# PEER experts: the gate pieces and early Gelu rows of pairs 2 and up requested from ScalarE's queue, value and up tiles alone on SyncE's

## The reference, cut to what matters

```python
    def one_block(args):
        xb, ib, gb = args
        u = expert_u[ib]
        a = jax.nn.gelu(jnp.einsum('thkd,td->thk', u, xb).astype(jnp.float32), approximate=False)
        w = (gb * a).astype(expert_v.dtype)
        return jnp.einsum('thk,thkd->td', w, expert_v[ib])
```

## Time and profile before

| | us |
|---|---|
| median of 3 runs | 2859.49 |
| lowest and highest | 2853.49, 2860.74 |
| the profiled execution's own time | 2859.18 |
| its span, first to last instruction | 2857.5 |
| TensorE busy | 2618.8 (92%) |
| VectorE busy | 2137.3 (75%) |
| ScalarE busy | 1347.5 (47%) |
| GpSimd busy | 887.8 (31%) |
| mean granted TensorE clock | 0.960 |
| stage `experts` in the span | about 748 to 1642 |

### The profile page before, as it was taken

How to read it: one execution, slowest core, us unless ns; L and a number is a source line. 1 busy time by engine, 2 the same in 40 slices (tenths; PEclk the granted TensorE clock), 3 DMA queues, 4 the chain that set the end, 5 groups by cost and what they waited for, 6 DMA issues and landing times. The chain is left out here.

```text
span 2857.5 us, 37085 instructions
## 1 busy us (share of the span) xinstructions
PE 2618.8 (92%) x12984; PEld 2188.0 (77%) x12984; DVE 2137.3 (75%) x3830; ACT 1347.5 (47%) x2125; POOL 887.8 (31%) x732
## 2 busy tenths in 40 slices
PE   4899989999999999999999969988898799999993
PEld 3656768888877999999988848857677688888883
DVE  4657658989677988888888866366434799999994
ACT  3224543547533333333333344343342688888882
POOL 2300024765433666554555510001000311122210
PEclk8999999999999999999999979999998899999997
DMA  7730011546899999999999922223222999999993
GB/s 238 263 119 1 30 61 60 181 142 240 317 314 323 356 368 368 372 349 352 349 350 353 329 70 89 89 89 107 89 69 74 295 399 381 370 373 371 366 357 117
DMA packets 278982, 681.49 MB, mean 238 GB/s; under 512 B 57892, under 2 KB 111908, under 8 KB 275752
## 3 DMA queue, kind: packets, MB, share of 16 engines
q1 hardware_dynamic: 219704, 480.26, 47.2%
q0 software_dynamic: 55664, 176.23, 17.3%
q10 hardware_dynamic: 3456, 23.07, 2.0%
HBM read 648.75 MB, written 55.84 MB: 247 GB/s over the span
## 5 line engine op out<-in xcount | busy, mean ns | idle before, releaser
L3381 ACT ACTIVATE ex_w_hi<-expert_raw 128x1024 fp32r<-128x1024 f32 x384 | 376.1, 1072 | 46.7 <-DMA expert_raw<-in_w 24.8
L2100 PE MATMUL bank<-v_hi,peer_w_hi 128*128 128x512 f32 x768 | 302.2, 394 | 12.5 <-DVE peer_w_lo L2203 12.4
L2075 POOL DMA_INDIRECT got_rows<-in_u_rows,diff x160 | 240.2, 1501 | 229.3 <-DVE got_rows L2169 192.0
L3427 DVE TENSOR_TENSOR ex_w_lo<-expert_raw,ex_w_hi 128x1024 fp32r<-128x1024 f32 x256 | 296.5, 1217 | 7.8 <-ACT ex_w_hi L3381 6.2
L2100 PE MATMUL bank<-v_lo,peer_w_hi 128*128 128x512 f32 x768 | 301.0, 392 | 0.0
L2100 PE MATMUL bank<-v_hi,peer_w_lo 128*128 128x512 f32 x768 | 300.6, 391 | 0.0
L2075 POOL DMA_INDIRECT got_rows<-in_expert_v,diff x160 | 218.2, 1364 | 201.5 <-DVE peer_acc L2174 154.4
L2088 PE MATMUL bank<-h_hi,u_hi 128*128 128x352 f32 x736 | 239.8, 326 | 8.4 <-PEq L94 4.9
L2088 PE MATMUL bank<-h_hi,u_lo 128*128 128x352 f32 x736 | 238.5, 324 | 0.0
L2088 PE MATMUL bank<-h_lo,u_hi 128*128 128x352 f32 x736 | 237.7, 323 | 0.0
L2141 ACT ACTIVATE v_hi<-v_in 128x1024 fp32r<-128x1024 f32 x128 | 133.0, 1058 | 211.5 <-PE bank L2100 117.4
(11 more groups left out here) (548 smaller groups left out, 6597.1 us busy)
## 6 DMA issues: line engine op xcount, KB each, us to landing
expert_raw<-in_w SPq DMA_DIRECT2D x384, 512.0 KB, 8.2
v_in<-in_expert_v SPq DMA_DIRECT2D x128, 512.0 KB
u_in<-in_u_tiles SPq DMA_DIRECT2D x118, 512.0 KB
ada_in<-in_w_ada SPq DMA_DIRECT2D x48, 512.0 KB, 4.9
ring<-in_w_in SPq DMA_DIRECT2D x11, 2048.0 KB, 8.6
gates_by_key<-spread ACTq DMA_DIRECT2D x20, 1024.0 KB, 8.3
gate_in<-gates_by_key SPq DMA_DIRECT2D x320, 64.0 KB
ring<-in_w_out SPq DMA_DIRECT2D x4, 2048.0 KB, 8.4
```

Of the source, the lines that this page charges most:

```text
L2075: pool.indirect_dma_start(out=got[:, n % RINGS, :], out_offset=None, in_=table, in_offset=bass.IndirectOffsetOnAxis(ap=rows_at[:, n % ROWS ...
L2100: last = pe.matmul(g.bank[2 + o][:, :], x[:, par, e, i * P:(i + 1) * P], v[par][:, e, c], start=(first and n == 0), stop=(final and i < FU ...
L3381: act.activation(hi[kind][:, c, :], raw_piece(raw, u * PIECES + c), ACT.Copy).then_inc(s["r_hi"], 1)
L3427: dve.tensor_tensor(lo[which][:, c, :], raw_piece(raw, u * PIECES + c), hi[which][:, c, :].bitcast(F32), ALU.subtract).then_inc(s["r_lo"], 1)
```

## The change

`gates_in` and `gel_ready` move out of the SyncE block and take the engine as an argument. SyncE still requests them for pairs 0 and 1. For pair `q + 2` they are requested by ScalarE at the end of its turn `q`, behind both `peer_w_hi` of pair `q`. The wait for `j_w` is gone, because ScalarE has at that point already waited for the same count.

```diff
+            def gates_in(eng, q):
+                for b in range(NB - 1):
+                    eng.dma_start(gate_in[:, q % 2, b], gates[b, :, q * GT:(q + 1) * GT, :]).then_inc(s[f"j_g{q % 2}"], 16)
+                eng.dma_start(gate_last[:, q % 2], last_gate[:, q * GT:(q + 1) * GT, :]).then_inc(s[f"j_g{q % 2}"], 16)
+
+            def gel_ready(eng, q):
+                eng.dma_start(gel_in[:, q % 2], early_gel[q * GT:(q + 1) * GT].rearrange("e p t -> p e t")).then_inc(s[f"j_e{q % 2}"], 16)
+
             @block.sync
...
-                def gates_in(q):
-                    if q >= 2:
-                        sp.wait_ge(s["j_w"], (q - 1) * GT)
...
                 early.saved(sp, EARLY)
-                gel_ready(0)
+                gel_ready(sp, 0)
                 last_gates(sp)
-                gates_in(0)
+                gates_in(sp, 0)
                 for q in range(1, Q):
                     down_in(q)
-                    gates_in(q)
-                    if q < EQ:
-                        gel_ready(q)
+                    if q == 1:
+                        gates_in(sp, q)
+                        gel_ready(sp, q)
                     if EQ <= q < Q - AHEAD:
                         up_in(q + AHEAD)
...
                         if EQ <= q < Q - AHEAD:
                             act_u(act, q + AHEAD, e)
+                    if q + 2 < Q:
+                        gates_in(act, q + 2)
+                    if q + 2 < EQ:
+                        gel_ready(act, q + 2)
                     if q == HALFWAY - 1:
```

## The result

The changed kernel takes 2873.37 us (median of 5 runs, 2870.11 to 2877.24), the kernel before 2858.57 in the same comparison (2853.49 to 2860.74). The ratio is 1.006 with an interval of 1.0043 to 1.0077: **slower by 0.6%**, some 15 us. The forecast was 2869, range 2855 to 2883. One execution of a later variant, behind_tiles, took 5328 us instead of some 2869 and is left out of its ratio.

A forecast was written before the change was run, and what follows sets the result against it. Early pairs were taken as bound by a loop through ScalarE, VectorE and value tiles, late pairs by full TensorE and VectorE. 2859.18 + 9.7 us of early ScalarE issuing, all else zero, gave 2869 us, range 2855 to 2883.

The forecast's parts named there:

- Case A: Early pairs: ScalarE's issuing closes the loop, 9.5 us a pair against 8.91, +9.7 us in all; chance 0.60.
- The block: Early pairs: seven requests on ScalarE between second `peer_w_hi` and first `v_hi`, taken as 3.7 us.
- The second part: Early pairs: from first `v_hi` to the next pair's second `peer_w_hi`, 5.7 us.
- The upper end of the block: Early pairs: the seven requests take 5 us if pieces cost 0.7 us, as when the queue is full.
- The loop before: Early pairs before the change: loop through ScalarE, VectorE and value tiles, 160.3 us for 18 steps, 8.91 each.
- the alternating pairs: Early pairs before the change: steps of 7.9 and 9.8 us in turn, the slow ones awaiting a value tile.
- The late pairs at zero: Late pairs: six requests, some 3.2 us, behind `u_hi` on ScalarE would cost nothing.
- The cover named: Late pairs: gathered rows hold VectorE's `v_lo` anyway, leaving 4 us to spare for ScalarE's delayed `v_hi`.
- SyncE's part at nothing: Removing gate and `gel_in` requests from SyncE gains nothing, since no engine waits for its issuing.
- B: Early pairs: value tiles land early, issuing fits idle time, loop falls to 8.3 us; -11 us, 2848; chance 0.12.
- C: Early pairs: earlier arrivals cancel the issuing cost, 9.0 to 9.2 us a pair, 0 to +5 us, 2862; chance 0.15.
- D: Early pairs: tiles come later or TensorE's clock falls during longer pauses; +15 to +30 us, 2882; chance 0.13.

The follow-up runs named there:

- behind_tiles: Changed kernel with the early pairs' requests moved behind ScalarE's two `v_hi` of a turn; 2869.4 us, ratio 1.0038 to the kernel before.
- early_only: Changed kernel with only the early pairs' requests on ScalarE, the late pairs' back on SyncE; 2871.3 us, ratio 1.004 to the kernel before.
- late_only: Changed kernel with the early pairs' requests back on SyncE, only the late pairs' on ScalarE; 2864.8 us, ratio 1.0021 to the kernel before.
- merged_five: Changed kernel with a pair's five gate pieces in one request, three requests per early pair instead of seven; 2861.1 us, ratio 1.0011 to the kernel before.
- sync_ahead: Changed kernel with the requests issued by SyncE instead of ScalarE, unmerged, at the same early moment; 2863.7 us, ratio 1.0014 to the kernel before.
- doubled: Changed kernel with the early pairs' gate pieces requested key by key, twelve requests a pair instead of seven; 2916.5 us, ratio 1.0197 to the kernel before.
- before_third: Third profile of the unchanged kernel before; early pairs 154.3 us, kernel median 2858.5 us.
- merged_early: merged_five with ScalarE requesting for the early pairs only, the late pairs' merged gates on SyncE; 2857.2 us, ratio 0.9993 to the kernel before.
- sync_merged: Kernel before with a pair's five gate pieces merged into one request on SyncE; 2856.6 us, ratio 0.9989 to the kernel before.
- after_again: Second profile of the changed kernel, nothing altered; early pairs 170.8 us, kernel median 2873.4 us.

## Why the prediction was right, and where its terms were off

**What bounds the early pairs, and the rival that came.** Case A happened by its own working. early_only has the loss with these requests alone. late_only, merged_five and sync_ahead lose it by taking requests off ScalarE, and doubled scales it. The issue time, moved to the engine that closes the loop, was nearly the whole price: 13.8 us of the 14.8. The Trainium skill, page "DMA: Bandwidth & Descriptors", section "Issuing engines are not separate DMA queues", calls the issue time that several issuing engines save usually small beside the DMA itself; here a block of seven took 3.4 to 4.8 us of a pair's 9.5.

**The block.** I took 3.7 us and a start 0.1 us after `peer_w_hi`, 3.8 to `v_hi`. It starts after 0.02 us and takes 3.7 on average; most blocks are 3.5 long, and single slow requests stretch some, up to 4.8. To `v_hi` it is 3.83 on average. The second part, 5.71 us, was right to 0.01. For the sixteen pairs with seven requests 9.5 us each was forecast, for all eighteen 170.0; measured 9.53 and 170.6. They are less alike than I had said: 9.24 to 10.65, eight of the sixteen between 9.3 and 9.7. The upper end of the block rested on pieces of 0.7 us with a full queue. No row shows a full queue; ScalarE's pieces in this stretch took 0.49 us on average and 1.84 at most.

**The loop before: the term that was mis-sized.** "8.91 us each" was one execution, and the slowest of three. Against their mean of 156.8 the early loss is 170.6 - 156.8 = 13.8 us, not 9.7. The landing of value tiles, by which I had explained the alternating pairs, is the part that varies: its waits were 32.8 us in that profile and 26.6 in before_third (this stretch's row):

```profile
ACT v_hi L2141 <- DMA v_in<-in_expert_v: 26.6, 21, 2.4
```

So I had taken a chance delay of the old loop for its length. That execution was also the only one of the three with a fall of the granted clock in this stretch. Its total lay at the median all the same, since its stage began at 748.3, 3.5 us ahead of the mean of the fourteen profiles. The sum ended 4.4 us under the measured median, inside the range: the 13.8 and a late loss of about 1 us make the measured 14.8.

**The late pairs at zero: wrong, and for another reason than the one named.** The cover named, 4 us ahead of `v_lo`, does hold: in pairs 18 to 38 of every profile `v_lo` waits for `v_hi` once, for 1.4 us. ScalarE's timeline of a late pair of after:

```profile
1481.86 0.48 ACT L2147 ACTIVATE peer_w_hi<-peer_w 128x352 fp32r<-128x352 f32 x1
1482.00 0.33 ACTq L2031 DMA_DIRECT2D gate_in<-gates_by_key  x1
1482.24 0.45 ACT L2127 ACTIVATE gel<-bank 128x352 f32<-128x352 f32 x1
1482.36 0.46 ACTq L2031 DMA_DIRECT2D gate_in<-gates_by_key  x1
1482.59 1.05 ACT L2121 ACTIVATE u_hi<-u_in 128x1024 fp32r<-128x1024 f32 x1
1482.84 1.60 ACTq L2031 DMA_DIRECT2D gate_in<-gates_by_key  x3
1484.47 0.45 ACTq L2032 DMA_DIRECT2D gate_last<-last_gates_by_key  x1
1485.03 1.06 ACT L2138 ACTIVATE v_hi<-v_in 128x1024 fp32r<-128x1024 f32 x1 [1.38 <-DMA v_in<-in_expert_v]
```

The requests do not stand behind `u_hi`, as I had put it: they go out beside `gel` and `u_hi`, and `v_hi` starts 3.17 us after `peer_w_hi`, hardly later than the 1469.13 - 1466.23 = 2.9 of before. What costs time are VectorE's waits for gathered rows. Pairs 18 to 38 take 312.6 to 320.4 us with these requests on ScalarE, 312.2 to 313.5 with them on SyncE; the two ranges overlap, and in after the cost is about 1 us (313.4 and 313.8 against 312.2 to 312.7). I had named the gathers as sharing the engines with the tiles, but had no term for them. That it is a third queue beside SyncE's and the gathers', and not the earlier moment, rests on sync_ahead, with 5 such waits. A rival is left: the number of requests on that queue. merged_five, with two requests a late pair in place of six, same queue and moment, has 11 such waits but only 8.0 us of them, and 312.6 us like before; no run separates the two. How the transfer engines share out their time between the queues no row shows, so this part is argued. The Trainium skill, page "DMA: Bandwidth & Descriptors", section "Queues, rings and completion order", has each transfer engine take turns between the queues. By that rule a third queue takes turns from the gathers; no run here shows the turns.

**SyncE and the value tiles.** SyncE's part at nothing was right as far as it was tested: early_only, which gives it the late gates back, is as slow as after within the intervals. The value tiles did come out of the way, 5.9 us of waits instead of 32.8, but because ScalarE came later for them. With three requests, in merged_five, ScalarE comes early again and waits for them 22 times, 25.9 us: with SyncE's queue free of gates the tiles are hardly earlier than in before_third (26.6 us), and the 153.5 us stand beside before's 154.3 to 160.3.

**The other rivals.** B wanted a block under 3.1 us and C one near 3.3; after's blocks of seven took 3.7 on average and 3.4 at least. merged_five and merged_early, with blocks of 1.5 us, are what B would have been, and even they gain nothing at the median that is clear of noise. Of D, TensorE's longest pauses grew to 2.2 and 2.3 us in the two profiles of after, and its granted clock stayed up in the stretch in both; doubled, with pauses of up to 4.6 us, shows the repeated fall.

## What to carry to other kernels

Before a request is put on an engine, ask whether that engine is in the loop that ends last. Seven requests held ScalarE for 3.7 us of a pair of 9.5, and the number of requests set the price, not their bytes: merge them first, then choose the engine. A loop bound by landings varies from run to run, so profile the kernel before two or three times before a length of one execution becomes a term of a sum. And a stage at the limit of its transfers (share 1.00) can pay for a second queue in somebody else's landings, here the gathered rows': about 1 us in after, up to 8 in late_only.

## What the runs showed of the hardware that was not expected

- One request with the rows of five took 0.38 us on ScalarE's queue, five requests 2.45.
- ScalarE's requests do not wait for the instructions ahead of them in its list to finish, nor even to start. In the early pairs they begin 0.02 us after the start of `peer_w_hi`; in the late pair shown above the first one begins at 1482.00, ahead of `gel` (1482.24) and `u_hi` (1482.59), which stand before it in the list. An instruction behind them waits for the last.
- The length of a single pause does not tell whether TensorE's granted clock falls. It fell to 0.50, its lower level of 1.2 GHz, during or within 1.5 us behind pauses of 1.83 us (sync_merged), 1.94 (after, just behind the early stretch), 2.29 (before), 2.40 (behind_tiles) and 2.45 (early_only). It stayed at 1.00, 2.4 GHz, behind pauses of 2.20 (after), 2.26 (after_again) and 2.31 (behind_tiles). So the two pauses of the earlier trace rows, on which rival D had built, do not carry a rule. The matmul behind a pause and the window after it (columns as in the earlier trace rows), two places of after:

```profile
884.97 0.50 PE L2097 MATMUL bank<-v_hi,peer_w_hi 128*128 128x512 f32 x1 [2.20 <-DVE peer_w_lo L2204]
885.00:887.00 2.00, 2.00 (x9) 1.66 (x10) 2.00 (x3) 0.00 (x0) 0.68 (x1) 1.00 0.54 163
```

```profile
942.18 0.48 PE L2085 MATMUL bank<-h_hi,u_hi 128*128 128x352 f32 x1 [1.94 <-DVE u_lo L2162]
942.40:945.80 3.40, 3.40 (x13) 3.40 (x13) 3.40 (x6) 2.10 (x2) 1.13 (x1) 0.50 0.96 302
```
